# Two products per token spread the gates, VectorE adds the parts, GpSimd makes the activations' low halves and 24 more table halves

## The reference

```python
    expert = i1 * N_SUBKEYS + i2
    gate = jax.nn.softmax(best_v, axis=-1).astype(h.dtype)
...
        u = jnp.take(u_tab, ex, axis=0)
        act = jax.nn.gelu(jnp.einsum('thkd,td->thk', u, hx), approximate=False) * gx
        vv = jnp.take(v_tab, ex, axis=0)
        return jnp.einsum('thk,thkd->td', act, vv)
```

## Time and profile before

| | before |
|---|---|
| median of 3 runs | 2271.77 us (2269.49 to 2275.51) |
| the profiled execution | 2269.8 us |
| its span | 2268.0 us, mean granted clock 0.983 |
| TensorE matmul busy | 2168.8 us (96%), 21816 products |
| VectorE busy | 1589.1 us (70%) |
| ScalarE busy | 1092.7 us (48%) |
| GpSimd busy | 336.4 us (15%) |

### The profile page before, as it was taken

One profiled execution on the slowest core, in us unless ns is written; L12 is line 12 of the kernel. 1 busy time (PEld: TensorE's weight loads), 2 busy tenths in 40 slices (PEclk: granted clock), 3 DMA queues, 4 the chain that ended last, 5 costly groups with the idle time before them and its releaser, 6 DMA issues.

```text
span 2268.0 us, 55219 instructions
## 1 busy us (share of the span) xinstructions
PE 2168.8 (96%) x21816; PEld 1945.1 (86%) x21816; DVE 1589.1 (70%) x3080; ACT 1092.7 (48%) x1881; POOL 336.4 (15%) x166
## 2 busy tenths in 40 slices
PE   8888999999999999999998889999999999999997
PEld 8877999988888888788787879999888888887885
DVE  6645797876666667975576448968766666679755
ACT  5533455444444444444464344554444444444443
POOL 0021697000000000000000226960000000000000
PEclk9999999999999999999999999999999999999998
DMA  6212345334444444445342133443344444444451
GB/s 253 93 41 85 139 167 185 130 130 166 166 166 167 166 166 167 148 165 188 136 149 86 41 112 136 180 167 132 135 167 167 166 167 167 167 159 149 167 201 66
DMA packets 46618, 335.04 MB, mean 148 GB/s; under 512 B 5168, under 2 KB 5296, under 8 KB 6320
## 3 DMA queue, kind: packets, MB, share of 16 engines
q1 hardware_dynamic: 46512, 333.61, 41.1%
HBM read 332.54 MB, written 1.05 MB: 147 GB/s over the span
## 4 chain that ended last, share of the span: by engine, by line
PE 79%; issue 6%; POOL 6%; DVE 6%; ACT 2%; DMA 1%; POOLq 0%; SPq 0%; DVEq 0%; ACTq 0%
PE PS L1648 31%; PE PS L1625 23%; PE PS L1310 8%; PE PS L1637 6%; POOL low L435 5%; PE PS L1326 3%; PE PS L1490 1%; DVE low L1084 1%; PE PS L1539 1%; PE PS L1528 1%; ACT high L459 1%; DVE hot L1154 1%; DMA ring<-in_w_slabs 1%; DVE hot L1150 1%; PE PS L1358 0%
## 5 line engine op out<-in xcount | busy, mean ns | idle before, releaser
L649 ACT CAST high<-ring 128x1024 fp32r<-128x1024 f32 x512 | 535.6, 1048 | 603.3 <-PE PS L1625 444.1
L1625 PE MATMUL PS<-hTh,high 128*128 128x256 f32 x2048 | 595.9, 291 | 13.0 <-ACT GA L653 10.9
L1625 PE MATMUL PS<-hTh,low 128*128 128x256 f32 x2048 | 579.6, 283 | 0.0
L1625 PE MATMUL PS<-hTl,high 128*128 128x256 f32 x2048 | 578.2, 282 | 0.0
L1084 DVE TENSOR_TENSOR low<-ring,high 128x1024 fp32r<-128x1024 f32 x432 | 515.4, 1220 | 0.9 <-ACT high L649 0.7
L1625 PEld LDWEIGHTS PS<-hTh,high 128*128 128x128 f32 x2048 | 387.9, 189 | 17.7 <-ACT GA L653 9.7
L1625 PEld LDWEIGHTS PS<-hTl,high 128*128 128x128 f32 x2048 | 388.4, 190 | 0.0
L1625 PEld LDWEIGHTS PS<-hTh,low 128*128 128x128 f32 x2048 | 388.2, 190 | 0.0
L1648 PE MATMUL PS<-high,WH 128*128 128x512 f32 x1024 | 324.2, 398 | 0.0
L1648 PE MATMUL PS<-low,WH 128*128 128x512 f32 x1024 | 318.4, 392 | 0.0
L1648 PE MATMUL PS<-high,WL 128*128 128x512 f32 x1024 | 316.7, 391 | 0.0
(11 more groups left out here) (251 smaller groups left out, 2992.1 us busy)
## 6 DMA issues: line engine op xcount, KB each, us to landing
ring<-in_peer_slabs SPq DMA_DIRECT2D x256, 1024.0 KB, 4.8
ring<-in_w_slabs SPq DMA_DIRECT2D x58, 1024.0 KB, 4.9
xres<-in_x SPq DMA_DIRECT2D x2, 512.0 KB, 4.5
out<-obuf SPq DMA_DIRECT2D x2, 512.0 KB, 2.6
cst<-in_consts SPq DMA_DIRECT2D x1, 680.0 KB, 10.4
praw<-in_p_t SPq DMA_DIRECT2D x1, 512.0 KB, 15.1
gfin<-in_g_final SPq DMA_DIRECT2D x1, 512.0 KB, 5.7
vec<-in_vecs SPq DMA_DIRECT2D x1, 356.0 KB, 7.3
```

The source lines that it names most:

```text
L649: act.copy(high[:, (c0[L] + j) % DEEP], ring[:, place, half * D:(half + 1) * D]).then_inc(part_hi, 1)
L1625: ins = mm(PS[:, 6 + j % 2, 0:SEQ], u[:, b, ks], h[:, k], start=n == 0, stop=n == 3 * KT - 1)
```

## The change

In chunks 0 to 2 a spread makes two products a token instead of three: one of 64 columns, which writes the gate's first two parts side by side, and one of 32 columns, which adds the third part to the second. VectorE then adds the two halves by a reduction of 512 elements out of PSUM into a new tile `gate_sum` in SBUF (`sum_gates`), and `apply_gates` multiplies `GA` with that tile. A spread waits for the sum two groups before (`gates_summed`) instead of the gates. Chunk 3 stays as it was (`last_spread`). In C `sum_gates` stands between VectorE's two `split_uv`.

`POOL_U` becomes 64: GpSimd also makes the low halves of the tiles 40 to 63, and SyncE's loads of these slabs wait for `low_pool`. All 128 `split_w` of a layer move from VectorE to GpSimd, behind the table halves in its queue. Nothing of the operation itself changes.

```diff
 POOL_WQ = HC - WQ_DVE
-POOL_U = A_LOOP
+POOL_U = HELD
 POOL_ALL = POOL_WQ + POOL_U
-DVE_U, DVE_V, DVE_ALL = HELD - POOL_U, 2 * NSUB - HELD, N_ALL - POOL_ALL
+DVE_V, DVE_ALL = 2 * NSUB - HELD, N_ALL - POOL_ALL
 C_UV, C_VV = HELD, 3 * HELD
...
     by_pool = stage == "wq" and k >= WQ_DVE
-    low = layer * POOL_ALL + k - WQ_DVE if by_pool else layer * DVE_ALL + first + k + (DVE_U + DVE_V - POOL_WQ) * peer
+    low = layer * POOL_ALL + k - WQ_DVE if by_pool else layer * DVE_ALL + first + k + (DVE_V - POOL_WQ) * peer
     return Tile(layer, slab + k // 2, k % 2, layer * N_ALL + first + k + 2 * NSUB * peer, low, by_pool)
...
         repeats = place("repeats", R + 22528, [2, 5, GROUP, REP], BF16)
+        gate_sum = place("gate_sum", R + 22848, [QT, GROUP])
...
         parts_made, repeated = sem("parts_made"), sem("repeated")
-        is_i2_made, hots_made, spread_ps, gated = (sem(n) for n in ("is_i2_made", "hots_made", "spread_ps", "gated"))
+        is_i2_made, hots_made, spread_ps, gates_summed, gated = (sem(n) for n in ("is_i2_made", "hots_made", "spread_ps", "gates_summed", "gated"))
         ga_ready, w_hi, w_lo, peer_ps = (sem(n) for n in ("ga_ready", "w_hi", "w_lo", "peer_ps"))
...
         c0 = [N_ALL * L + N_PRE for L in range(DEPTH)]
-        d0 = [DVE_ALL * L + N_EARLY for L in range(DEPTH)]
-        v0 = [d + DVE_U for d in d0]
+        v0 = [DVE_ALL * L + N_EARLY for L in range(DEPTH)]
         u0 = [POOL_ALL * L + POOL_WQ for L in range(DEPTH)]
...
                         load(L, j, peer_slabs[L, RING * i + (j + RING)])
-                with sp.Fori(0, DVE_U // (2 * RING)) as i:
-                    for j in range(RING):
-                        sp.wait_ge(low_dve, d0[L] + 2 * (RING * i + j) + 2)
-                        load(L, j, peer_slabs[L, RING * i + (j + POOL_U // 2 + RING)])
...
                         split_tile(j % 2, j // 2 % RING, c0[L] + 8 * i + j, j)
+                def split_w(s, at, j):
+                    pool.wait_ge(w_hi, NSUB * L + 1 + s)
+                    pool.tensor_tensor(WL[:, j % 2:j % 2 + 1], GA[:, bass.ds(at, 1)], WH[:, j % 2:j % 2 + 1].bitcast(F32), ALU.subtract).then_inc(w_lo, 1)
+                for place in (0, HELD):
+                    with pool.Fori(0, HELD // 8) as i:
+                        for j in range(8):
+                            split_w(8 * i + (j + place), 8 * i + j, j)
                 norm(3 * L + 2)
...
+                def sum_gates(g, b):
+                    dve.wait_ge(spread_ps, g0 + 1 + g)
+                    dve.tensor_reduce(gate_sum[:], PS[:, 4 + b].rearrange("p (t q i) -> p i t q", t=GROUP, q=2), AX.X, ALU.add).then_inc(gates_summed, 1)
                 def apply_gates(g, group, b, chunk):
-                    dve.wait_ge(spread_ps, g0 + 1 + g)
                     acts = GA[:, chunk % 2 * QT:chunk % 2 * QT + QT, bass.ds(GROUP * group, GROUP)]
-                    dve.tensor_tensor(acts, acts, PS[:, 4 + b, 0:GROUP * QT].rearrange("p (t i) -> p i t", t=GROUP), ALU.mult).then_inc(gated, 1)
-                def split_w(s, place, j):
-                    dve.wait_ge(w_hi, NSUB * L + 1 + s)
-                    dve.tensor_tensor(WL[:, j % 2:j % 2 + 1], GA[:, bass.ds(place, 1)], WH[:, j % 2:j % 2 + 1].bitcast(F32), ALU.subtract).then_inc(w_lo, 1)
-                def split_uv(s, j):
-                    split_tile(2 * s + C_UV, 2 * j, j % RING, 0)
-                    split_tile(2 * s + (C_UV + 1), 2 * j + 1, j % RING, 1)
+                    if chunk < NQ - 1:
+                        dve.wait_ge(gates_summed, sums + 1 + g)
+                        dve.tensor_tensor(acts, acts, gate_sum[:], ALU.mult).then_inc(gated, 1)
+                    else:
+                        dve.wait_ge(spread_ps, g0 + 1 + g)
+                        dve.tensor_tensor(acts, acts, PS[:, 4 + b, 0:GROUP * QT].rearrange("p (t i) -> p i t", t=GROUP), ALU.mult).then_inc(gated, 1)
+                def split_uv(s, j, v):
+                    split_tile(2 * s + (C_UV + v), 2 * j + v, j % RING, v)
...
-                def split_u(e):
-                    split_tile(e, e, e // 2 % RING, e % 2)
+                sums = NGROUPS * (NQ - 1) * L
                 one_hots(0, 0, 0)
-                for e in range(POOL_U, POOL_U + 2):
-                    split_u(e)
...
                     one_hots(g + 1, (b + 1) % 2, int(last))
+                    sum_gates(g, b)
                     apply_gates(g, g, b, 0)
...
                 for e in range(A_LOOP, HELD):
-                    if e < HELD - 2:
-                        split_u(e + 2)
                     for g in spreads_after(e):
                         first_chunk(g, g % 2, g == NGROUPS - 1)
-                split_uv(0, 0)
-                split_w(0, 0, 0)
+                for v in range(2):
+                    split_uv(0, 0, v)
...
                     one_hots(s + (NGROUPS + 1), (j + 1) % 2, chunk + last)
-                    split_uv(s + 1, j + 1)
+                    split_uv(s + 1, j + 1, 0)
+                    sum_gates(s + NGROUPS, j % 2)
+                    split_uv(s + 1, j + 1, 1)
                     apply_gates(s + NGROUPS, group, j % 2, chunk)
-                    split_w(s + 1, s + 1, j + 1)
...
                         one_hots(s + NGROUPS + 1, 0, 3)
+                        sum_gates(s + NGROUPS, 1)
                         apply_gates(s + NGROUPS, s % QT, 1, 2)
-                        split_w(s + 1, 0, 0)
                 dve.wait_ge(ga_ready, NSUB * (L + 1))
...
                     apply_gates(n + (HELD + NGROUPS), n, j % 2, 3)
-                    split_w(n + (HELD + 1), n + 1, j + 1)
...
                         split_vv(8 * i + (j + 1), j + 1)
-                        split_w(8 * i + (j + HELD + 1), 8 * i + (j + 1), j + 1)
                 for j in range(7):
                     split_vv(HELD - 8 + j + 1, j + 1)
-                    split_w(NSUB - 8 + j + 1, HELD - 8 + j + 1, j + 1)
                 for k in range(4):
...
-                def hidden(e, j, b, second=False, by_dve=False):
+                def hidden(e, j, b, second=False):
...
                         pe.wait_ge(low_dve, v0[L] + 1 + 2 * (e - HELD))
-                    elif by_dve:
-                        pe.wait_ge(low_dve, d0[L] + 1 + (e - POOL_U))
                     else:
...
+                sums = NGROUPS * (NQ - 1) * L
                 def spread(g, b):
...
-                    if L or not isinstance(g, int) or g > 1:
+                    if not isinstance(g, int) or g > 1:
+                        pe.wait_ge(gates_summed, sums - 1 + g)
+                    elif L:
                         pe.wait_ge(gated, g0 - 1 + g)
+                    for t in range(GROUP):
+                        at = 2 * t * QT
+                        mm(PS[:, 4 + b, at:at + 2 * QT], hot1[:, b, t], hot2[:, b, 0:2, t], start=True, stop=False, skip_group_check=True)
+                        ins = mm(PS[:, 4 + b, at + QT:at + 2 * QT], hot1[:, b, t], hot2[:, b, 2, t], start=False, stop=True, skip_group_check=True)
+                    ins.then_inc(spread_ps, 1)
+                def last_spread(g, b):
+                    pe.wait_ge(hots_made, g0 + 1 + g)
+                    pe.wait_ge(gated, g0 - 1 + g)
                     for t in range(GROUP):
...
                 for e in range(A_TOP, A_LOOP + 4):
-                    hidden(e, e, e, by_dve=e >= POOL_U)
+                    hidden(e, e, e)
                     if e in (A_LOOP, A_LOOP + 2):
...
                     for j in range(4):
-                        hidden(4 * i + (j + A_LOOP + 4), j, j, by_dve=True)
+                        hidden(4 * i + (j + A_LOOP + 4), j, j)
                         spread(6 * i + (2 + 3 * j // 2), 3 * j // 2 % 2)
...
                     for j in range(4):
-                        spread(4 * i + (j + NGROUPS), j % 2)
+                        last_spread(4 * i + (j + NGROUPS), j % 2)
                         spend(4 * i + j, j, j, low_dve, v0[L] + (HELD + 1) + 4 * i + j)
...
```

## The result

The changed kernel takes 2316.13 us (2311.18 to 2320.62, 4 runs) against 2273.64 for the kernel before on the same chip (four runs, the three of the first table among them): a ratio of 1.0202, 95% interval 1.0183 to 1.0221. It is slower by 42 us. The profiled execution has a span of 2315.2 us, 47 more than that of before.

The account below looks back on a forecast made before the run. TensorE was taken to bound C and E, with VectorE close in B. C's -21.8 and B's +51.2 over both layers gave +29.4 us on the profiled execution, so 2300 us, with a range of 2256 to 2334.

Parts of the forecast that it names:

- C: Stage of 64 steps of spread, hidden, spend, where TensorE sets the pace: shorter spreads save 21.8 us over both layers.
- A: Stage of `hidden` 0 to 39, with low halves by GpSimd, ahead of stage B: claimed to stay as before.
- B, the port: Stage of 24 `hidden` and 32 `spread`: VectorE operations with two SBUF inputs and GpSimd's take turns, +25.6 us a layer.
- the start: Start of stage B, from VectorE's first decoding cast to the first product of hidden 48: +8.9 us a layer.
- the six half blocks: Middle of stage B, two hiddens and three spreads each, with GpSimd's tiles 52 to 63: 11.1 us each, +18.3 a layer.
- the last four tiles: Last two half blocks of stage B, without GpSimd's tiles: -0.8 us each, -1.6 a layer.
- The clock: Rival, chance 0.16: TensorE's waits in stage B lower the granted clock and slow the hiddens, +24 us, giving 2324.
- The spread's term: Stage C: the 64-column product takes 30 ns, so a spread costs 445 ns in place of 614 on TensorE.
- C's cover, D and E: VectorE's added sum fits the steps of C (at most 5.3 of 6.1 us); later stages D and E lose nothing.
- Relief: Rival, chance 0.14: short bf16 operations avoid the port or GpSimd's tiles fall into VectorE's pauses; B becomes TensorE's, 2228.
- Full cover: Rival, chance 0.10: in stage B every sum and wait lies under port work, +15 us for both layers, about 2268.
- C as VectorE's: Rival, chance 0.03: VectorE sets the pace in stage C, needing 0.8 us more blocking in each step; 2310.

Follow-up runs that it names:

- fill_in_b: The changed kernel with GpSimd filling the low halves of tiles 40 to 63 with zeros, reading nothing, in place of subtracting; 2244.6 us.
- warm_in_b: The changed kernel with five products of zeros on TensorE before the second spread after each fourth tile of stage B; 2300.9 us.
- tiles_alone: The kernel before with only the 24 table halves moved to GpSimd; 2279.0 us, ratio 1.0030 to the kernel before.
- two_in_c: The kernel before with two products a token and the sum only in chunks 1 and 2 (stage C); 2262.1 us, ratio 0.9958.
- wl_alone: The kernel before with only the activations' low halves moved to GpSimd; 2271.7 us, ratio 1.0002 to the kernel before.
- c_and_24_tiles: The kernel before with two products a token in stage C only and all 24 tiles on GpSimd; 2267.8 us, ratio 0.9992.

## Why the prediction was right

**The sign and the size.** 2300 was forecast, with 2256 to 2334, and +29 on the profiled execution; measured 2316 and +42 without the difference ahead of A. Slower had 0.73.

**B, the port.** The step was +25.6 a layer; measured +28.0 and +28.2, with the part that fell into A (below) 29.0 and 29.4. (Its upper end was given as +29; the terms add up to +28.) The mechanism was right, also where no row had shown it (bf16 one-hots, gates out of SBUF), and fill_in_b shows it alone. The Trainium skill ("SBUF — State Buffer", Who interferes with whom) says that a VectorE instruction with two SBUF inputs contends with a GpSimd instruction that reads SBUF, not with one that only writes it; the trace agrees, 2.62 us beside a subtraction and 0.43 beside a fill.
The sum was right partly by luck: without dips of the clock, in warm_in_b, the stretch of the step (first cast to hidden 64) is 22.3 longer than before, and the clock, which the step left out, put 7 on top. By terms: the start was +6.3 in place of +8.9; the six half blocks +20.6, in warm_in_b +15.9, in place of +18.3; the last four tiles +2.4 and +0.2 in place of -1.6. The half block of 11.1 us is 10.7 in warm_in_b, where nothing but VectorE and the port holds B, and 11.2 to 11.8 in the changed kernel. VectorE's sum of the gates stood at 0.60 us and costs 0.71 where the gates follow at once; and VectorE lost 7.7 of GpSimd's 9.5 us in a block, a little less than the 8.9 I had used. GpSimd itself lost little: its subtractions in B took 2.5 us, not the 3 or more that I had named as a sign. "Turns for the whole length" is an upper bound where VectorE has pauses: in tiles_alone the same reckoning gave +12 and the measured was +4.7. It holds where VectorE has none, as after the change.

**The clock.** Named as a rival with 0.16 and +24. It was no rival but a part: dips to 0.5 in every block, 6.9 us a layer by warm_in_b, about 14 of the 42. A granted clock of 0.5 within B was one of my own signs of being wrong, and it came; the sign was badly chosen, since the waits of the port bring the dips with them. The forecast's range took the clock in, its centre left it out. The stages came to +43.6 where +29.4 was forecast: the clock is 14 of that gap and C 7, and the port's terms, summed 7 too high, hid half of the clock.

**C.** -21.8 was forecast for both layers, measured -14.8, and steps of 6.13 us, measured 6.19. The spread's term held: 30 ns for the 64-column product, measured 28 to 29 (39 for the first of a spread); the spread 0.17 shorter, measured 0.161. Timeline of TensorE, changed kernel:

```profile
636.75 0.20 PE L1640 MATMUL PS<-hot,hot 128*128 128x64 bf16 x1
636.79 0.18 PE L1641 MATMUL PS<-hot,hot 128*128 128x32 bf16 x1
636.82 0.19 PE L1640 MATMUL PS<-hot,hot 128*128 128x64 bf16 x1
636.85 0.18 PE L1641 MATMUL PS<-hot,hot 128*128 128x32 bf16 x1
```

The formula of the Trainium skill ("TensorE: Matmul & The Clock Gate", Back-to-back issue gap) would have had 29.2; the trace agrees to within a nanosecond. What failed is "what leaves TensorE's queue leaves the time": hidden and spend of the same step became 0.034 and 0.020 us longer, so 0.107 of the 0.161 were left. two_in_c ties this to the new spread and not to GpSimd. Why 256-column products start 1.5 ns further apart is open.

**C's cover, D and E.** VectorE is busy for 322 of 393 us in C (busy time counts its waits) and is not late: steps are 6.19 throughout. D and E didn't move, and wl_alone moved nothing: both covers held.

**A.** Given as unchanged: where GpSimd subtracts for tiles behind 39, the first spread comes 1 us later (A is 126.3 to 126.7 in the seven such kernels, 125.2 to 125.6 in the other five, fill_in_b among them), since GpSimd goes on while VectorE decodes. I had the mechanism inside B's first term, which counts from the first cast, still in A.

**The rivals.** Relief: wrong as the change was made, but fill_in_b (2244.6, 2228 forecast) is what it would have been without turns. Full cover: tiles_alone and c_and_24_tiles come near it, since there the sums are not in B. C as VectorE's: no, steps are 6.19 and TensorE doesn't wait.

## What to carry to other kernels

Before work goes to an idle GpSimd, ask whether it reads SBUF and whether VectorE then runs operations with two SBUF inputs without a pause: if so, GpSimd's time is added to VectorE's nearly in full (here 81%), and what VectorE sheds (1.1 us a tile) is less than what it waits (1.9). It costs less while VectorE has pauses (24 tiles +4.7 us a stage, eight nothing that can be told), and an operation that takes one input from PSUM or that reduces isn't held off. Two changes can each look cheap (here +4.7 and +11 us a stage) and cost 28 together, because the first uses up the slack that hid the second; and an engine that begins to wait in each block can lose its clock too, so put a price on it in the sum, not beside it. A saving on TensorE is worth taking only in the stage where TensorE is last: two products in C alone gave what the change was worth.

## What the runs showed of the hardware

- A GpSimd fill of 128 x 1024 float32 (0.95 us) runs beside VectorE's two-input operations with no loss on either side; a subtraction of the same size (2.39 us) holds them off until it is through (gates 2.62 us in place of 0.43), and a VectorE reduction or a product with one input in PSUM is not held off (0.69 and 0.40 us beside it).
- Changing the spread from 24 products of 32 columns to 16 of 64 and 32 made the unchanged 256-column products behind it, in C, start 123.6 ns apart in place of 122.1 and the 512-column ones 231.5 in place of 229.7; in D, with the old spread, both kernels have 239.0.
- In B of the changed kernel the granted clock fell to a half once in each block and once at the end, 27 of 121 us in all, each time while TensorE stood idle for 2.0 to 3.6 us; 2 us of products of zeros in the gap of each block were enough to keep the clock at 1.00.
